# Handing the last two forward tiles of each head to the backward sweep in on-chip buffers instead of through memory

## The chip, the cores and the metric

The kernel runs on all 8 cores of one Trainium2 chip. Each core computes one sequence of the batch of 8, with the same program and no exchange between cores. The metric is the device time of the slowest core in microseconds (us).

## The reference

One hybrid encoder block on x of shape (8, 4096, 1024), float32:

```
h = adaLN(RMSNorm(x)); z = h @ W_in
hA = mlstm_scan(q, k, v, forward gates) + flip(mlstm_scan(flipped q, k, v, backward gates))   # 4 heads of 256
y  = sigmoid(gA) * (rmsnorm(hA) * mh_g * sigmoid(o)) + sigmoid(gB) * spatial_gating(u, v)
x += gate1 * (y @ W_out)
x += gate2 * (relu(adaLN(RMSNorm(x)) @ W1)^2 @ W2);  out = RMSNorm(x)
```

What matters here is the first line of the mixer: a head's output is the sum of a forward scan and a backward scan over the same 4096 positions, and the root-mean-square norm comes after that sum.

## The kernel before, in words

The sequence is cut into 32 tiles of 128 positions. The program has three stages. The first (to about 480 us in the profile) normalises, transposes and does the spatial gating branch. The second, the head stage (about 480 to 1320 us), does the mLSTM of the four heads. The third is the channel sub-layer with its two large matrix products; it goes through the tiles from the last to the first, and its first pieces of work are mixed into the end of the head stage.

The head stage is a loop over `t`, 0 to 159, and every turn of it calls `chunk_pair`. In turn t the forward scan of head `hF = t // 32` does tile `iF = t % 32`, and the backward scan of the head before, `hB = hF - 1`, does tile `iB = 31 - t % 32`. So in the first 32 turns there is only a forward scan (pass 1), in passes 2 to 4 there are both, and in the last 32 turns (pass 5) only a backward scan. The point where `t` reaches 32, 64, 96 or 128 is called a hand-over below: tile 31 of a head is the last one that its forward scan makes and the first one that its backward scan needs, one turn later. Tile 30 is made one turn earlier and needed one turn later than that.

Inside one `chunk_pair`:

- `recur("F", ...)` writes the forward numerators into PSUM bank 4 with TensorE, updates the state `Chat` on VectorE and its scaled bf16 copy `Cbf` on ScalarE. `recur("B", ...)` does the same for the backward scan with bank 5 (its `Cbf` on GpSimd, in pass 5 on ScalarE).
- For the backward tile, TensorE also makes the output gates into bank 3 from the weights `wog` (1 MB per head, loaded by `load_og`), ScalarE takes a tanh, and GpSimd makes the product `y2`.
- VectorE makes the reciprocals of the denominators of both directions with two operations and a RECIPROCAL (L1085 to L1087).
- Line 1090: ScalarE scales bank 4 by the reciprocal into the buffer `hfo[t % 2]` (float32, 128x256). Line 1091: SyncE's queue stores it to `hf_d`, in memory (128 KB).
- Line 1059: SyncE's queue loads the forward result of the backward tile from `hf_d` into `hfi[t % 3]` (128 KB).
- Line 1093: VectorE adds bank 5, scaled, to `hfi[t % 3]`, giving `hs`. ScalarE squares it (L1096, into `mxo`), GpSimd makes the reciprocal root, VectorE makes the product `mxo` (L1099), and SyncE's queue stores `mxo` to `mixa_d` (L1101).

Beside each turn, TensorE, VectorE and ScalarE do a quarter of a block of the projections of the coming blocks (`prep_part`), through pass 4. In pass 5 there are no projections left.

The order of the instructions on each engine isn't the order of the source. A planner (`Sched.schedule`) gives each operation an assumed duration and places it by the time at which its inputs are ready in that assumed time, earliest rank first among those that are ready. The ranks follow the source. A DMA is assumed to take 3 us plus its bytes at 280 GB/s, and transfers of one queue follow each other. The order so found is fixed in the program; on the chip each engine works through its own list and waits wherever an input isn't there yet. Waits are written as semaphore waits ahead of the instruction, on SyncE's queue as well. A planned order depends on all planned times before it.

Helpers record nearly all operations, so the lines of the profile are theirs: L354 is every DMA, L361 every matmul group, L373 transposes, L381 every activation, L393 and L392 tensor-scalar, L396 tensor-tensor, L401 scalar-tensor-tensor. A wait instruction has L1409 (for a DMA) or L1411 (for another engine).

Of the kernel before, what the change touches and what calls it, by code (L numbers as in the profile page):

```python
# [10 lines left out]
AF = mybir.ActivationFunctionType  # L11
# [31 lines left out]
class Sched:  # L43
# [8 lines left out]
    def R(self, *key):  # L52
        r = self.res.get(key)
        if r is None:
            r = Res(key)
            self.res[key] = r
        return r
# [188 lines left out]
def build_program(debug=False):  # L246
    nc = bass.Bass("TRN2", target_bir_lowering=False)
    SCH = Sched()
    R = SCH.R
# [33 lines left out]
    hf_d = [nc.dram_tensor(f"hf{j}_d", [S, 256], F32, kind=sk).ap() for j in range(2)]  # L283
# [8 lines left out]
    with es:  # L292
        arena = es.enter_context(nc.sbuf_tensor("arena", [128, ARENA_WORDS], F32))
        ps_all = es.enter_context(nc.psum_tensor("ps", [128, 4096], F32))[:, :]
        banks = [ps_all[:, i * 512:(i + 1) * 512] for i in range(8)]
# [3 lines left out]
        def new_dsem():  # L299
            nsem[0] += 1  # L300
            return DSem(es.enter_context(nc.semaphore(f"dsem{nsem[0]}")))
# [5 lines left out]
        def alloc(shape, dt=F32, res=(), at=None):  # L307
            n = 1
            for s_ in shape[1:]:
                n *= s_  # L310
            nb = (n * (4 if dt == F32 else 2) + 31) // 32 * 32
            if at is None:
                off = ptr[0]
                ptr[0] += nb
            else:
                off = at
            assert off + nb <= ARENA_WORDS * 4, ("arena overflow", off + nb)
            keys = [k if isinstance(k, tuple) else (k,) for k in res]
            old = []
            for r in regions:  # L320
                if r[0] < off + nb and off < r[1]:
                    assert r[2] and keys, ("no owner", shape, r)
                    old += r[2]
            regions.append((off, off + nb, keys))
            if old:
                SCH.alias(old, keys)
            ap = arena[:, off // 4:(off + nb) // 4]
            if dt != F32:
                ap = ap.bitcast(dt)
            ap = ap[:, 0:n]  # L330
            if len(shape) == 3:
                ap = ap.rearrange("p (a b) -> p a b", a=shape[1], b=shape[2])
            return ap
# [4 lines left out]
        def PB(i):  # L338
            return R("bank", i)

        def nfree(ap):
            n = 1
            for s_ in ap.shape[1:]:
                n *= s_
            return n
# [4 lines left out]
        def DMA(q, o_ap, i_ap, reads, writes, sem, pace=(), **kw):  # L350
            if q == "pool" and sem is None:
                sem = new_dsem()
            nbytes = nfree(o_ap) * o_ap.shape[0] * (4 if o_ap.dtype == F32 else 2)
            return SCH.op(q, lambda e, o_ap=o_ap, i_ap=i_ap, kw=kw: e.dma_start(out=o_ap, in_=i_ap, **kw),  # L354
                          reads, writes, dsem=sem, pace=pace, occ=0.4 if q == "sp" else 0.9, lat=3.0 + nbytes / (280e3 if q == 'sp' else 100e3))
# [22 lines left out]
        def ACTF(o_, i_, func, reads, writes, eng="act", **kw):  # L378
            t = 0.17 + nfree(o_) * 0.000833 + (0.19 if "accum_out" in kw else 0.0)
            t += 0.093 * sum(not isinstance(kw.get(n_, 1.0), float) for n_ in ("scale", "bias"))  # L380
            return SCH.op("act", lambda e, o_=o_, i_=i_, func=func, kw=kw: e.activation(o_, i_, func, **kw),  # L381
                          reads, writes, occ=t)
# [12 lines left out]
        def TT(eng, o_, a_, b_, op, reads, writes):  # L395
            return E(eng, lambda e, o_=o_, a_=a_, b_=b_, op=op: e.tensor_tensor(o_, a_, b_, op), reads, writes,  # L396
                     0.6 if op == ALU.pow else vcost(eng, o_))
# [41 lines left out]
        def hTt(kc, i):  # L439
            return hT4[:, i // 4, kc, (i % 4) * 128:(i % 4 + 1) * 128]  # L440
# [3 lines left out]
        def RH(i):  # L444
            return R("hT", i)
# [179 lines left out]
        def gpart(i):  # L625
            return int(i >= 28)
# [244 lines left out]
        hfo = [alloc([128, 256], F32, [("hfo", k)]) for k in range(2)]  # L871
        hfo_sem = [new_dsem() for _ in range(2)]
        hfi = [alloc([128, 256], F32, [("hfi", k)]) for k in range(3)]
        hfi_sem = [new_dsem() for _ in range(3)]
# [5 lines left out]
        sml = alloc([128, NSM * 8], F32, [(nm, m) for nm in ("sml", "sq") for m in range(NSM)])  # L880
# [7 lines left out]
        def RHF(hh_, i):  # L888
            return R("hf_d", hh_ % 2, i)
# [12 lines left out]
        BV, BOG, BN, BD = 2, 3, {"F": 4, "B": 5}, 6  # L902
# [144 lines left out]
        def chunk_pair(hF, iF, hB, iB):  # L1047
            t = pctr[0]
            pctr[0] += 1
            k2 = t % 2  # L1050
            so = (t % NSM) * 8
            RSM = R("sml", t % NSM)
            if hF is not None:
                recur("F", hF, iF)
            if hB is not None:
                bsl = slice(iB * 128, (iB + 1) * 128)
                k3 = t % 3
                DMA("sp", hfi[k3], hf_d[hB % 2][bsl, :], [RHF(hB, iB)], [R("hfi", k3)], hfi_sem[k3])
                recur("B", hB, iB)
                MMG([(banks[BOG][:, 0:512], hTt(kc, iB), wog[:, kc, :], kc == 0, kc == 7) for kc in range(8)],  # L1060
                    [RH(iB), R("wog")], [PB(BOG)])
                RT = R("tg", k2)
                ACTF(tg[k2], banks[BOG][:, 0:512], AF.Tanh, [PB(BOG)], [RT], scale=0.5)
                TS("dve" if hF is None else "pool", tg[k2], tg[k2], 0.5, 0.5, ALU.mult, ALU.add, [RT], [RT])
                TT("pool", y2[k2], tg[k2][:, 0:256], tg[k2][:, 256:512], ALU.mult, [RT], [R("y2", k2)])
                TT("pool", y2[k2], y2[k2], mhs[hB % 2], ALU.mult, [R("y2", k2), R("mhs", hB % 2)], [R("y2", k2)])
            iB = None if hB is None else iB
            iF = None if hF is None else iF
            aF = None if hF is None else iF * 4 + hF
            aB = None if hB is None else 128 + iB * 4 + hB  # L1070
            if aF is None:
                den, wvn, n_ = banks[BN["B"]][:, 256:257], wvi[:, aB:aB + 1], 1
                rb = [PB(BN["B"])]
                dn, rd = sml[:, so + 1:so + 2], sml[:, so + 3:so + 4]
            elif aB is None:
                den, wvn, n_ = banks[BN["F"]][:, 256:257], wvi[:, aF:aF + 1], 1
                rb = [PB(BN["F"])]
                dn, rd = sml[:, so:so + 1], sml[:, so + 2:so + 3]
            else:
                b0 = BN["F"] * 512  # L1080
                den, wvn = ps_all[:, b0 + 256:b0 + 256 + 513:512], wvi[:, aF:aB + 1:aB - aF]
                rb = [PB(BN["F"]), PB(BN["B"])]
                dn, rd = sml[:, so:so + 2], sml[:, so + 2:so + 4]
            STT(dn, den, -1.0, wvn, ALU.mult, ALU.max, rb + [R("gsc", "w", gpart(i_)) for i_ in (iF, iB) if i_ is not None], [RSM])
            STT(dn, den, 1.0, dn, ALU.mult, ALU.max, rb + [RSM], [RSM])  # L1085
            E("dve", lambda e, o_=rd, i_=dn: e.reciprocal(o_, i_), [RSM], [RSM], 0.2)  # L1086
            if hF is not None:  # L1087
                fsl = slice(iF * 128, (iF + 1) * 128)
                ACTF(hfo[k2], banks[BN["F"]][:, 0:256], AF.Copy, [PB(BN["F"]), RSM], [R("hfo", k2)], scale=sml[:, so + 2:so + 3])
                DMA("sp", hf_d[hF % 2][fsl, :], hfo[k2], [R("hfo", k2)], [RHF(hF, iF)], hfo_sem[k2])  # L1090
            if hB is not None:
                STT(hs[k2], banks[BN["B"]][:, 0:256], sml[:, so + 3:so + 4], hfi[k3], ALU.mult, ALU.add,
                    [PB(BN["B"]), RSM, R("hfi", k3)], [R("hs", k2)])
                RS2 = R("sq", t % NSM)
                ACTF(mxo[k2], hs[k2], AF.Square, [R("hs", k2)], [R("mxo", k2), RS2], accum_out=sml[:, so + 4:so + 5])
                TS("pool", sml[:, so + 5:so + 6], sml[:, so + 4:so + 5], 1.0 / 256.0, EPS, ALU.mult, ALU.add, [RS2], [RS2])  # L1096
                RSTD(sml[:, so + 5:so + 6], sml[:, so + 6:so + 7], RS2, RS2)
                STT(mxo[k2], hs[k2], sml[:, so + 6:so + 7], y2[k2], ALU.mult, ALU.mult,
                    [R("hs", k2), RS2, R("y2", k2)], [R("mxo", k2)])  # L1099
                DMA("sp", mixa_d[bsl, hB * 256:(hB + 1) * 256], mxo[k2], [R("mxo", k2)], [R("mixa_d", iB, hB)], mxo_sem[k2])  # L1100

        casts = []
        for j in range(2):
            for m in range(2):
# [391 lines left out]
```

How the kernel before makes its waits and increments, by code:

```python
    def replay(e, h):  # L1405
        for o in order[e]:
            for d in o.waits:
                if d.dsem is not None:
                    h.wait_ge(d.dsem.handle, d.dval)
                else:
                    h.wait_ge(esem[d.eng], d.count)
            if o.fn is None:
                if o.signal:
                    h.nop().then_inc(esem[e], 1)
                continue
            ins = o.fn(h)
            if o.dsem is not None:
                ins.then_inc(o.dsem.handle, 16)
            elif o.signal:
                ins.then_inc(esem[e], 1)
```

## Time and profile before

| | us |
|---|---|
| median of 3 runs | 2346.45 (2344.16 to 2347.35) |
| the profiled execution, its own time | 2342.24 |
| its span, core 0 (slowest) | 2340.7 |
| the other cores' spans | 2332.2 to 2339.1 |
| granted TensorE clock, mean of each core | 0.980 to 0.982 |
| TensorE matmul busy | 2211.5 |
| VectorE busy | 1414.3 |
| ScalarE busy | 1134.6 |
| GpSimd busy | 923.3 |

The span runs from the first to the last instruction of a core. The rows shown further down are all of core 0. Its own time is 1.5 us more than its span and lies 4.2 us below the median of the runs.

### The profile page before, as it was taken

To read this page: it belongs to the slowest core of one execution; us is meant where nothing else is said; L and a number is where in the kernel's file an instruction comes from. 1 tells how busy PE (TensorE), PEld (TensorE's weight loads), DVE (VectorE), ACT (ScalarE), POOL (GpSimd) and SP (SyncE) were. 2 spreads that over 40 slices of the span, in tenths; PEclk is the share of its full clock that TensorE was granted. 3 is DMA by queue.
4 is the path that set the end of the run, shared out by engine and by line. 5 is a ranking of instruction groups with operands and counts; after the bars stand their busy time and mean duration, and the time that the engine had idled before them with its cause. 6 is when DMAs were issued, how large, how long until landed. Compare 5 with 4: busy or idle time off the path is not lost.

```text
span 2340.7 us, 49311 instructions; the slowest of 8 cores (2332.2 to 2340.7 us)
## 1 busy us (share of the span) xinstructions
PE 2211.5 (94%) x15044; PEld 1337.3 (57%) x15044; DVE 1414.3 (60%) x3077; ACT 1134.6 (48%) x2291; POOL 923.3 (39%) x1153
## 2 busy tenths in 40 slices
PE   5999999999999999999868999999999999999997
PEld 1454545555666555555524566666666666666664
DVE  2768887788888778888758533343333343434433
ACT  4645554488766566666635333333333333333332
POOL 1656666111576566666656412222112222221220
PEclk7999999999999999999989999999999999999998
DMA  9544444224334544544565511110111111111100
GB/s 306 176 120 138 131 122 127 77 51 100 82 76 102 117 97 104 144 100 98 146 184 184 178 55 55 55 32 33 55 55 55 47 55 55 55 55 55 41 7 35
DMA packets 109265, 219.96 MB, mean 94 GB/s; under 512 B 15687, under 2 KB 65415, under 8 KB 102158
## 3 DMA queue, kind: packets, MB, share of 16 engines
q1 hardware_dynamic: 105006, 187.16, 25.3%
q0 software_dynamic: 4000, 29.66, 8.2%
q8 instruction: 124, 2.03, 0.4%
q14 instruction: 135, 1.11, 0.2%
HBM read 196.08 MB, written 79.71 MB: 118 GB/s over the span
## 4 chain that ended last, share of the span: by engine, by line
PE 76%; DVE 8%; issue 6%; DMA 4%; POOL 3%; ACT 2%; SPq 1%; DVEq 0%; POOLq 0%; ACTq 0%
PE ps L361 74%; DVE arena L401 5%; POOL arena L396 2%; PE ps L373 2%; ACT arena L381 1%; DMA arena<-x 1%; DVE arena L396 1%; DMA arena<-w_ada 1%; DMA arena<-wg_d 1%; SPq L354 1%; DMA mixa_d<-arena 1%; DVE arena L656 0%; DMA arena<-wsT 0%; POOL arena L393 0%; DVEq L1411 0%
## 5 line engine op out<-in xcount | busy, mean ns | idle before, releaser
L361 PE MATMUL ps<-arena 128*128 128x256 bf16 (+6 forms) x14020 | 2168.1, 321 | 95.6 <-DVE arena L401 34.7
L361 PEld LDWEIGHTS ps<-arena 128*128 128x128 bf16 (+1 forms) x14020 | 1276.4, 98 | 946.8 <-issue 183.9
L396 POOL TENSOR_TENSOR arena<-arena 128x1 f32<-128x1 f32 (+3 forms) x647 | 694.4, 1081 | 1056.4 <-ACT arena L381 353.9
L401 DVE SCALAR_TENSOR_TENSOR arena<-ps,arena 128x256 bf16<-128x256 f32 (+6 forms) x1474 | 606.4, 414 | 615.7 <-ACT arena L381 480.0
L381 ACT ACTIVATE arena<-ps 128x256 f32<-128x256 f32 (+2 forms) x974 | 495.2, 522 | 837.7 <-PE ps L361 702.0
L381 ACT ACTIVATE arena<-arena 128x256 bf16<-128x256 f32 (+6 forms) x566 | 405.4, 725 | 244.6 <-DVE arena L401 92.5
L381 ACT ACTIVATE arena<-ps,arena 128x512 f32<-128x512 f32 (+3 forms) x512 | 252.3, 519 | 106.6 <-DVE arena L396 31.3
L401 DVE SCALAR_TENSOR_TENSOR arena<-arena 128x256 bf16<-128x256 f32 (+4 forms) x259 | 277.9, 1074 | 30.9 <-POOL arena L396 17.9
L396 DVE TENSOR_TENSOR arena<-ps,arena 128x512 bf16<-128x512 f32 (+4 forms) x298 | 170.8, 580 | 106.1 <-PE ps L361 102.1
L393 POOL TENSOR_SCALAR arena<-arena 128x1 f32<-128x1 f32 (+2 forms) x317 | 152.8, 483 | 143.5 <-ACT arena L381 107.3
L401 DVE SCALAR_TENSOR_TENSOR arena<-arena,ps 128x514 f32<-128x514 f32 x240 | 178.7, 745 | 27.7 <-PE ps L361 24.8
L373 PE MATMUL ps<-arena 128*128 128x128 bf16 x1024 | 80.4, 223 | 17.7 <-POOL arena L396 7.7
L373 PEld LDWEIGHTS ps<-arena 128*128 128x128 bf16 x1024 | 67.1, 100 | 40.2 <-issue 22.0
L393 DVE TENSOR_SCALAR arena<-arena 128x1 f32<-128x1 f32 (+1 forms) x128 | 35.4, 278 | 60.2 <-ACT arena L381 60.0
L396 DVE TENSOR_TENSOR arena<-arena 128x2 f32<-128x2 f32 (+4 forms) x170 | 63.1, 373 | 11.7 <-ACT arena L381 3.4
L354 POOL DMA_DIRECT2D wq_d<-w_qkv x48 | 25.9, 540 | 84.1 <-DVE arena L1086 37.4
L656 DVE BATCH_NORM_STATS2 arena<-arena 128x6 f32<-128x512 f32 x64 | 44.2, 690 | 24.5 <-ACT arena L381 24.2
L392 DVE TENSOR_SCALAR arena<-arena 128x1 f32<-128x1 f32 (+5 forms) x72 | 31.0, 430 | 19.8 <-DMA arena<-bsp 12.6
L381 ACT ACTIVATION_READ_ACCUMULATOR arena<-arena 128x1 f32 x226 | 42.7, 189 | 0.0
L393 DVE TENSOR_SCALAR arena<-ps,arena 128x128 bf16<-128x128 bf16 x128 | 37.7, 337 | 2.1
L971 POOL CAST arena<-arena 128x4 bf16<-128x4 f32 x64 | 13.4, 223 | 64.6 <-DVE arena L396 37.7
L1086 DVE RECIPROCAL arena<-arena 128x2 f32<-128x2 f32 (+1 forms) x160 | 26.3, 164 | 15.3 <-DVE arena L401 0.9
(17 smaller groups left out, 90.3 us busy)
## 6 DMA issues: line engine op xcount, KB each, us to landing
arena<-x SPq DMA_DIRECT2D x64, 512.0 KB, 4.9
arena<-w_ada SPq DMA_DIRECT2D x8, 2048.0 KB, 11.5
hf_d<-arena SPq DMA_DIRECT2D x128, 128.0 KB, 3.4
arena<-hf_d SPq DMA_DIRECT2D x128, 128.0 KB, 2.9
w_d<-w POOLq DMA_DIRECT2D x32, 512.0 KB, 6.4
out<-arena SPq DMA_DIRECT2D x30, 512.0 KB, 3.5
arena<-w_d SPq DMA_DIRECT2D x13, 1024.0 KB, 5.6
arena<-w_vum SPq DMA_DIRECT2D x12, 1024.0 KB, 16.8
```

Source lines behind the costliest of these rows:

```text
L354: return SCH.op(q, lambda e, o_ap=o_ap, i_ap=i_ap, kw=kw: e.dma_start(out=o_ap, in_=i_ap, **kw), reads, writes, dsem=sem, pace=pace, occ=0 ...
L361: ins = e.matmul(o_, l_, r_, start=st, stop=sp)
L373: ins = e.transpose(o_, i_, ident)
L381: return SCH.op("act", lambda e, o_=o_, i_=i_, func=func, kw=kw: e.activation(o_, i_, func, **kw), reads, writes, occ=t)
L392: return E(eng, lambda e, o_=o_, i_=i_: e.tensor_scalar(o_, i_, s1, None, op0), reads, writes, t)
L393: return E(eng, lambda e, o_=o_, i_=i_: e.tensor_scalar(o_, i_, s1, s2, op0, op1), reads, writes, t)
L396: return E(eng, lambda e, o_=o_, a_=a_, b_=b_, op=op: e.tensor_tensor(o_, a_, b_, op), reads, writes, 0.6 if op == ALU.pow else vcost(eng, ...
L401: e.scalar_tensor_tensor(o_, a_, sc, b_, op0, op1), reads, writes, vcost("dve", o_))
L656: E("dve", lambda e, o_=st2[:, sb + hh * 6:sb + hh * 6 + 6], i_=gv[kv][:, cs]: e.bn_stats(o_, i_), [R("gv", kv, hh)], [R("st2", i % 4, hh) ...
L971: E("pool", lambda e, o_=vS[nm][k_][:, :, 256], i_=gsc["u" + nm][:, c0:c0 + 13:4]: e.tensor_copy(o_, i_), [R("gsc", "u", int(b == 7))], [R ...
L1086: E("dve", lambda e, o_=rd, i_=dn: e.reciprocal(o_, i_), [RSM], [RSM], 0.2)
```

## The change

For tiles 30 and 31 of each head, the forward result is no longer stored to `hf_d` and loaded back. ScalarE writes it directly into the `hfi` buffer that the backward scan of the next pass reads. The activation itself is the same (bank 4 scaled by the reciprocal) and moves to the end of `chunk_pair`, behind the operations of the backward tile in rank. It is no longer tied to the buffers `hfo` and their stores, but to the chosen `hfi` buffer and whoever read it last. For tile 30 of heads 1 to 3 the chosen buffer is the one that the backward sum of the same turn reads. The loads and stores of all other tiles stay.

```diff
             if hB is not None:
                 bsl = slice(iB * 128, (iB + 1) * 128)
                 k3 = t % 3
-                DMA("sp", hfi[k3], hf_d[hB % 2][bsl, :], [RHF(hB, iB)], [R("hfi", k3)], hfi_sem[k3])
+                if iB < 30:
+                    DMA("sp", hfi[k3], hf_d[hB % 2][bsl, :], [RHF(hB, iB)], [R("hfi", k3)], hfi_sem[k3])
                 recur("B", hB, iB)
...
             if hF is not None:
                 fsl = slice(iF * 128, (iF + 1) * 128)
-                ACTF(hfo[k2], banks[BN["F"]][:, 0:256], AF.Copy, [PB(BN["F"]), RSM], [R("hfo", k2)], scale=sml[:, so + 2:so + 3])
-                DMA("sp", hf_d[hF % 2][fsl, :], hfo[k2], [R("hfo", k2)], [RHF(hF, iF)], hfo_sem[k2])
+                if iF >= 30:
+                    turn_f.append((hF, iF, so, RSM))
+                else:
+                    ACTF(hfo[k2], banks[BN["F"]][:, 0:256], AF.Copy, [PB(BN["F"]), RSM], [R("hfo", k2)], scale=sml[:, so + 2:so + 3])
+                    DMA("sp", hf_d[hF % 2][fsl, :], hfo[k2], [R("hfo", k2)], [RHF(hF, iF)], hfo_sem[k2])
...
+            while turn_f:
+                hF_, iF_, so_, RSM_ = turn_f.pop()
+                kd = (32 * (hF_ + 1) + 31 - iF_) % 3
+                ACTF(hfi[kd], banks[BN["F"]][:, 0:256], AF.Copy, [PB(BN["F"]), RSM_], [R("hfi", kd)], scale=sml[:, so_ + 2:so_ + 3])
+
+        turn_f = []
```

## Rows read from the trace of the kernel before

**Rows 1.** The page: busy time by engine, the clock slices, and the end chain.
```profile
PE 2211.5 (94%) x15044; PEld 1337.3 (57%) x15044; DVE 1414.3 (60%) x3077; ACT 1134.6 (48%) x2291; POOL 923.3 (39%) x1153
...
PE 76%; DVE 8%; issue 6%; DMA 4%; POOL 3%; ACT 2%; SPq 1%; DVEq 0%; POOLq 0%; ACTq 0%
```
**Rows 2.** Windows of passes 2 to 4: window, length, busy us by engine, clock, DMA.
```profile
620.00:785.00 165.00, 162.53 (x1099) 99.48 (x1097) 138.80 (x310) 111.86 (x228) 116.82 (x209) 1.00 0.44 100
...
805.00:980.00 175.00, 164.43 (x1107) 100.32 (x1104) 141.03 (x315) 113.58 (x233) 110.56 (x199) 0.99 0.48 109
...
1000.00:1170.00 170.00, 158.97 (x1044) 95.38 (x1042) 136.82 (x304) 111.47 (x230) 110.89 (x198) 0.99 0.50 115
```
**Rows 3.** Windows around the four hand-overs, same columns.
```profile
600.00:620.00 20.00, 19.78 (x133) 12.24 (x134) 17.03 (x41) 14.60 (x30) 10.14 (x20) 1.00 0.40 89
...
788.00:803.00 15.00, 14.82 (x86) 8.31 (x87) 10.49 (x27) 9.16 (x20) 8.57 (x17) 0.89 0.45 97
990.00:1005.00 15.00, 15.00 (x100) 8.92 (x99) 11.88 (x24) 9.56 (x19) 7.93 (x15) 1.00 0.63 130
1184.00:1199.00 15.00, 10.88 (x52) 4.44 (x51) 6.37 (x16) 4.30 (x10) 4.88 (x9) 0.96 0.46 146
```
**Rows 4.** Tile hf_d: its DMA issues (ns min/median/max), and who waited for them.
```profile
L354 SPq DMA_DIRECT2D hf_d<-arena x128: 319/383/4067, 489.1 to 1189.6; - x128
L354 SPq DMA_DIRECT2D arena<-hf_d x128: 319/320/2561, 600.5 to 1305.8; - x128
...
  ACT arena L381: 5.2, 1
  DVE arena L401: 2.8, 1
```
**Rows 5.** Chain of waits at the fourth hand-over: start us, us, what.
```profile
1168.28 13.79 DMA arena<-wg_d
...
1189.62 5.90 DMA hf_d<-arena
...
1195.66 2.48 DMA arena<-hf_d
```
**Rows 6.** Timeline there: start us, us, engine, line, operation, shapes, [idle before <-releaser].
```profile
1182.20 6.11 PE L361 MATMUL ps<-arena 128*128 128x512 bf16 x25 [4.02 <-DMA arena<-wg_d]
1182.51 0.47 ACT L381 ACTIVATE arena<-ps,arena 128x256 f32<-128x256 f32 x1 [5.25 <-DMA hf_d<-arena]
...
1183.17 0.42 ACT L381 ACTIVATE arena<-arena 128x256 bf16<-128x256 f32 x1 [0.18 <-DMA mixa_d<-arena]
...
1187.17 0.47 ACT L381 ACTIVATE arena<-ps,arena 128x256 f32<-128x256 f32 x1 [0.99 <-DVE arena L1086]
...
1188.44 0.42 ACT L381 ACTIVATE arena<-arena 128x256 bf16<-128x256 f32 x1 [0.80 <-DMA mixa_d<-arena]
...
1189.29 0.16 DVE L1086 RECIPROCAL arena<-arena 128x1 f32<-128x1 f32 x1
...
1198.22 0.48 DVE L401 SCALAR_TENSOR_TENSOR arena<-ps,arena 128x256 f32<-128x256 f32 x1 [2.81 <-DMA arena<-hf_d]
...
1198.85 0.49 PE L361 MATMUL ps<-arena 128*128 128x257 bf16 x3 [1.94 <-DVE arena L401]
```
**Rows 7.** Windows from the fourth hand-over on, same columns as rows 2.
```profile
1188.00:1209.00 21.00, 13.60 (x56) 5.46 (x56) 11.43 (x30) 7.67 (x18) 8.86 (x16) 0.84 0.53 170
1209.00:1230.00 21.00, 15.95 (x94) 7.60 (x92) 16.61 (x45) 10.68 (x25) 13.79 (x24) 1.00 0.57 171
1230.00:1310.00 80.00, 70.55 (x400) 37.09 (x401) 67.89 (x165) 44.55 (x103) 53.58 (x84) 0.98 0.56 179
```
**Rows 8.** Timeline of the second hand-over, ScalarE and VectorE.
```profile
784.12 0.42 ACT L381 ACTIVATE arena<-arena 128x256 bf16<-128x256 f32 x1 [3.09 <-DMA mixa_d<-arena]
...
789.02 0.46 ACT L381 ACTIVATE arena<-ps,arena 128x256 f32<-128x256 f32 x1
789.45 0.42 ACT L381 ACTIVATE arena<-arena 128x256 bf16<-128x256 f32 x1
```

## The prediction

> **What bounds the kernel now.** Read the page's busy times and its end chain first: TensorE is busy for 94% of the span and carries 76% of the chain [rows 1]. So a change pays only where TensorE stands idle, and the question is where that is. The windows over the head stage answer it. Passes 2, 3 and 4 leave TensorE idle for 165 - 162.53 = 2.5 us, 175 - 164.43 = 10.6 us and 170 - 158.97 = 11.0 us [rows 2]. Then look at the four hand-overs, the only places that the change touches. In their windows TensorE is idle for 0.22 us of 20, 0.18 of 15, 0.00 of 15 and 4.12 of 15 [rows 3]. The first three have the store and the load too, but projections of coming blocks fill the time; the fourth opens pass 5, which has no projections left. The tile view says the same from the other side: of 256 stores and loads of `hf_d`, two were ever waited for by an engine, a ScalarE activation for 5.2 us and a VectorE sum for 2.8 us [rows 4], and the timeline puts both at the fourth hand-over [rows 6]. Last, the chain of waits there goes through the store (5.90 us) and the load (2.48 us) of tile 31 [rows 5].
>
> **The change part by part.**
>
> *Eight stores and eight loads go* (4 heads, 2 tiles). That is 16 x 128 KB = 2 MB of the head stage's traffic and 16 issues of 0.32 to 0.38 us on SyncE's queue [rows 4], about 5.5 us of a queue that isn't the bound. I count 0 for them by themselves. What matters is who waits.
>
> *Hand-overs 1 to 3: 0 us.* With the store and load gone, the sum of tile 31 can run some microseconds sooner. TensorE had at most 0.22 us idle there, so all three together can give back 0.22 + 0.18 + 0.00 = 0.4 us at most. I take 0.
>
> *Hand-over 4, the wait for tile 31.* The store was issued at 1189.62 and landed 5.90 us later, the load was issued at 1195.66 and took 2.48 us, and the sum ran at 1198.22, after VectorE had idled 2.81 us for it [rows 5, 6]. What else does that sum need? Its reciprocal, at 1189.29 for 0.16 us [rows 6], and bank 5, which the reciprocal's own inputs read before. So without the round trip it can run at about 1189.6, or 1198.22 - 1189.6 = 8.6 us sooner. That is the ceiling of this step. It isn't the gain, because TensorE went on working during the wait (output gates of coming tiles, which need only `hT` and `wog`), and this work is no longer available afterwards.
>
> The gain comes from TensorE's window. From 1188 to 1209 it was busy 13.60 of 21 us; the two stretches behind it, with the same kind of turns, were busy 15.95 of 21 (76%) and 70.55 of 80 (88%) [rows 7]. The same 13.60 us of work at those densities takes 13.60 / 0.76 = 17.9 or 13.60 / 0.88 = 15.4 us: 3.1 or 5.6 us less than 21. The granted clock was 0.84 in this window against 1.00 and 0.98 behind it [rows 7], TensorE having idled ahead. 0.84 as a mean of the full and the half level means that 32% of the stretch ran at 1.2 GHz; if that were all undone, a sixth of 13.60 us, 2.2 us at most, would come on top, but the idle time for `wog` stays (below), so I take a third, 0.7 us. Ends: 3.1 and 5.6 + 2.2 = 7.8, both under the ceiling of 8.6. I take 5.0, the middle of 3.1 and 5.6 with the 0.7.
>
> *Hand-over 4, the wait for an old store.* ScalarE waited 5.25 us until 1182.51 to write tile 30's result, because `hfo` was still being stored [rows 6]. This wait goes. Nothing is gained: TensorE stood still until 1182.20 for `wog` [rows 6], a transfer issued at 1168.28 [rows 5] ahead of everything that the change removes, and the next activation in the list, the square into `mxo`, ran at 1183.17 because its own buffer's store was late by the same congestion [rows 6]. That one is next late. Count 0; the ends are 0 and 0.6 us (1183.17 - 1182.51).
>
> *The copy moves behind the backward tile.* The activation is the same 0.46 to 0.47 us [rows 6, 8]. For tile 30 it now also waits for the sum of the same turn (0.48 us, [rows 6]) since that reads the same buffer, and by rank it comes behind the square of that turn. At the second hand-over copy and square ran back to back at 789.02 and 789.45 [rows 8], so swapping them makes bank 4 free some 0.4 to 0.6 us later. The next forward tile's matmuls wait for bank 4 and can be hidden behind projections, as TensorE's idle time there is near 0. Behind the copy on ScalarE are the `Cbf` copies and tanhs; they are moved in time only by what the planner places between. At the fourth hand-over the copy of tile 31 ran at 1187.17; behind the square at 1188.44 (0.42 us and its accumulator read) it would run at about 1189.1 and end at 1189.6 [rows 6], just as the reciprocal is done. So 0 there too. Price if the cover goes: 0.5 us a hand-over, 1.5 us in all; if the square waits for its buffer's store, up to 3.09 us (784.12, [rows 8]) each.
>
> *The planner's order.* Sixteen operations with assumed times of some 3.5 us disappear, so from the first hand-over on every engine's list may come out differently. The trace of before can't show this. The nearest rows are passes of the same work in other orders: their idle times of TensorE differ by up to 11.0 - 2.5 = 8.5 us [rows 2]. So -8.5 to +8.5 us, and I take 0, since nothing in the rows gives it a sign.
>
> **Sum.** -0 - 5.0 - 0 + 0 + 0 = -5.0 us against the profiled execution's own 2342.24: 2337.2. Its own time lies 4.2 us below the median of the runs, 2346.45, so on that scale the forecast is 2341.4 us. A difference under 0.2% (4.7 us) can't be told from no change here; the forecast lies just beyond that line.
>
> The Trainium skill bears on the price of the round trip. Here the store took 5.90 us and the load 2.48 us, 8.38 together [rows 5]. The page DMA: Bandwidth & Descriptors, section Anatomy of one DMA, gives about 2.0 us fixed plus the bytes at 436 GB/s, which for 128 KB would be an estimate of 2.3 us each and 4.6 us together. The load agrees, the store doesn't. By the page's price tile 31's sum would come at most 4.6 us sooner, and with the same discount for work done during the wait the result would be about 2344, within what can't be told from no change; the trace has the longer time, so it decides.
>
> **Rivals.**
>
> *A: given back within pass 5.* The last pass ends where VectorE and the weights' loads allow it, and the start hardly matters. For it: behind the hand-over VectorE is as busy as TensorE, 16.61 of 21 and 67.89 of 80 us (79% and 85%), and the loads of `hf_d` run on at (1305.8 - 1195.7) / 31 = 3.6 us a tile, near a pace of its own [rows 4, 5, 7]. At that pace the five tiles from 1187 on end at about 1205, when they really ended by 1209 or so: 2 to 4 us of gain remain, and later waits take more. Against it: VectorE isn't over 85% busy. Time on the median's scale: 2344 to 2347, no change measurable.
>
> *B: the new order is worse (slower).* From the first hand-over on the planner interleaves projections and scans differently, and TensorE meets its inputs late as in passes 3 and 4 rather than as in pass 2. Place: pass 2, from 620 to 785 us, the only one with an order this tight. Price: up to 8.5 us [rows 2]; it decides once the loss exceeds the 5.0 us of the hand-over by 4.7, which asks for more than this pass alone, so for a loss in pass 5 too. Time: 2352.
>
> *C: ScalarE's list (slower too).* The copy sits behind a square that waits for the store of `mxo`. Three hand-overs with 3.09 us each [rows 8] are 9.3 us less the 5.0: 2351. It decides only where such a wait meets the very turn with tile 30; in the rows of before it was one turn earlier. The page TensorE: Matmul & The Clock Gate of the Trainium skill, specification table ahead of the first section, has ScalarE's queue as strictly first in first out, so nothing could overtake the square; the ACT rows at 1182.51 and 1183.17 agree.
>
> *D: more than forecast.* The sum freed at 1189.6 keeps the clock up and the new order removes part of the 10.6 and 11.0 us of passes 3 and 4 as well: 8.6 us at the hand-over plus 2 to 4: 2335.
>
> **How the numbers follow.** Forecast 0.45 (itself spread over 3 to 8 us, a fifth of it under the line of 4.7), A 0.27, B 0.11, C 0.04, D 0.13. Faster by over 0.2%: 0.45 x 0.8 + 0.13 = 0.49. Same: 0.09 + 0.27 = 0.36. Slower: 0.15. The range goes from D's 2335, a little under, to 2350, which takes in A and the near half of B and C: 2334 to 2350. The forecast alone would be 2338 to 2344.
>
> **What would show it.** In the changed kernel the stores and loads of `hf_d` are 120 each, no wait of VectorE for them at the fourth hand-over, and the chain there no longer goes through `hf_d`. TensorE's wait for `wog` of about 4 us stays. The window of 21 us from the first matmul of pass 5 on should be busy 16 us or more with the clock near 1.0. The windows of hand-overs 1 to 3 should stay within 0.5 us. Passes 2 to 4 should be as long as before within 2 us each; if one is longer or shorter by more, the order did it (B, D). If the sum of tile 31 comes 8 us earlier, but the last load of `hf_d` less than 2 us earlier, it is A. The prediction is wrong if the hand-over returns nothing, or if passes 2 to 4 move by more than it.

## The result, and the profile after

The changed kernel takes 2324.1 us (median of 4 runs, 2320.1 to 2324.8) against 2345.3 us before. The ratio is 0.9908, with a 95% interval of 0.9892 to 0.9924: 21 us faster. The prediction said 2341.4, 5 us faster, and its range ended at 2334. The sign was right; the size was a quarter of the real one. In one run or another some executions were disturbed on one die; they are left out of all comparisons here, which is why a few kernels rest on few runs, and why the stages of one kernel below (the changed one with a reciprocal reckoned at 0.25 us) are those of its four undisturbed cores.

The page of the changed kernel, core 0, answers to [rows 1]: busy time, and the chain that ended last.

```profile
span 2323.0 us, 48997 instructions; the slowest of 8 cores (2314.0 to 2323.0 us)
...
PE 2185.5 (94%) x14771; PEld 1335.7 (57%) x15044; DVE 1401.3 (60%) x3077; ACT 1136.6 (49%) x2291; POOL 923.1 (40%) x1153
...
PE 79%; DVE 8%; issue 6%; DMA 2%; ACT 2%; POOL 1%; SPq 1%; DVEq 0%; ACTq 0%; POOLq 0%
```

The share of DMA in the chain fell from 4% to 2%. (273 matmul records are missing in this trace, so its idle times are slightly too long.) The tile view of `hf_d`, against [rows 4]:

```profile
L354 SPq DMA_DIRECT2D hf_d<-arena x120: 319/384/2312, 485.8 to 1173.3; - x120
L354 SPq DMA_DIRECT2D arena<-hf_d x120: 319/320/3866, 597.7 to 1292.5; - x120
its engine sat idle before it (us, times) until:
who waited for it (us, times):
```

There are 120 stores and 120 loads, and on this core no engine waits for any of them (on the others there are two such waits, of 1.0 and 2.5 us, both of ScalarE). Then the windows, against [rows 3] and [rows 7]: the four hand-overs, pass 5 in two parts, and the 60 us behind it (columns: busy time of TensorE, its weight loads, VectorE, ScalarE, GpSimd; clock; DMA).

```profile
600.00:620.00 20.00, 19.89 (x133) 12.21 (x134) 16.62 (x40) 13.96 (x28) 11.59 (x20) 1.00 0.32 62
786.00:801.00 15.00, 13.18 (x85) 7.54 (x85) 11.33 (x30) 9.43 (x22) 9.57 (x18) 1.00 0.49 119
985.00:1000.00 15.00, 14.89 (x91) 8.17 (x92) 9.89 (x23) 9.72 (x20) 7.52 (x15) 1.00 0.37 75
1184.00:1199.00 15.00, 11.67 (x61) 5.65 (x63) 12.18 (x33) 8.47 (x21) 8.83 (x17) 1.00 0.56 173
...
1187.00:1210.00 23.00, 17.17 (x96) 8.43 (x99) 19.54 (x56) 12.69 (x28) 15.27 (x26) 1.00 0.62 195
1210.00:1301.00 91.00, 80.81 (x465) 42.85 (x471) 73.77 (x190) 50.78 (x121) 64.13 (x100) 0.98 0.55 174
1301.00:1361.00 60.00, 57.63 (x388) 38.65 (x396) 21.56 (x55) 17.24 (x46) 10.57 (x11) 0.97 0.39 116
```

The same stretches of the kernel before, from the first turns of pass 5 on:

```profile
1189.00:1224.00 35.00, 24.12 (x114) 10.31 (x114) 22.06 (x57) 14.37 (x32) 16.71 (x32) 0.90 0.59 184
1224.00:1316.00 92.00, 79.39 (x457) 41.84 (x458) 77.99 (x187) 50.30 (x117) 64.41 (x98) 0.98 0.52 166
1316.00:1376.00 60.00, 58.16 (x385) 37.86 (x384) 21.34 (x53) 16.36 (x45) 8.56 (x12) 0.94 0.37 118
```

The first eight turns of pass 5 took 35 us and now take 23. In them TensorE is idle for 5.8 instead of 10.9 us, and its granted clock is 1.00 instead of 0.90. Of the prediction's signs, the 21 us from the first matmul of pass 5 on (1187.07) are busy for 16.24 us at a clock of 1.00, as it asked. The window of hand-over 2 didn't stay within 0.5 us: TensorE is idle there for 1.8 instead of 0.2 us (core 0).

To cut the whole span into stages, take the start of the RECIPROCAL of each turn (160 of them in every trace). The table has the median over the 8 cores of each kernel's profiled execution, in us. The last two rows are TensorE's idle time and the time at the half clock (1.2 GHz) for the two main kernels.

| stage | before | after | difference |
|---|---|---|---|
| up to turn 0, pass 1 (turns 0 to 32) | 604.2 | 604.5 | +0.3 |
| pass 2 (32 to 64) | 193.2 | 193.5 | +0.3 |
| pass 3 (64 to 96) | 197.7 | 194.1 | -3.6 |
| pass 4 (96 to 128) | 190.1 | 189.9 | -0.2 |
| turns 128 to 136 | 35.4 | 22.8 | -12.6 |
| turns 136 to 159 | 92.4 | 91.3 | -1.1 |
| the rest | 1022.6 | 1020.0 | -2.6 |
| TensorE idle, in pass 3 / turns 128 to 136 / whole | 10.8 / 11.1 / 129 | 4.9 / 5.5 / 116 | -5.9 / -5.6 / -13 |
| half clock, in turns 128 to 136 / next 60 us after pass 5 / whole | 8.5 / 4.6 / 90 | 0 / 0 / 78 | -8.5 / -4.6 / -12 |

13 us less idle time, and 12 us less at the half clock (worth at most half of that, 6 us), make 19 of the 19.5 us that the stages add up to. 12.6 of them lie right behind the fourth hand-over, where the prediction looked. But it looked for 5. (The expectations below give pass 4 a gain of 3.2 us as well; the medians over the cores don't show it.)

### The profile page after: what moved, and what is told of

Read it like the earlier page. It is cut to its first block, busy times and chain, and to the rows that moved or that the text cites. A ratio compares the mean times of both kernels' runs of the same rounds, so it can differ in the third digit from the quotient of the medians.

```text
span 2323.0 us, 48997 instructions; the slowest of 8 cores (2314.0 to 2323.0 us)
## 1 busy us (share of the span) xinstructions
PE 2185.5 (94%) x14771; PEld 1335.7 (57%) x15044; DVE 1401.3 (60%) x3077; ACT 1136.6 (49%) x2291; POOL 923.1 (40%) x1153
## 4 chain that ended last, share of the span: by engine, by line
PE 79%; DVE 8%; issue 6%; DMA 2%; ACT 2%; POOL 1%; SPq 1%; DVEq 0%; ACTq 0%; POOLq 0%
PE ps L361 77%; DVE arena L401 5%; PE ps L373 2%; ACT arena L381 2%; DVE arena L396 1%; DMA arena<-w_ada 1%; POOL arena L396 1%; DMA mixa_d<-arena 1%; SPq L354 1%; DMA arena<-wg_d 1%; DVE arena L393 0%; DVEq L1421 0%; DVE arena L1087 0%; POOL arena L393 0%; DVE arena L656 0%
## 5 line engine op out<-in xcount | busy, mean ns | idle before, releaser
L361 PE MATMUL ps<-arena 128*128 128x512 bf16 (+7 forms) x13747 | 2141.2, 318 | 107.5 <-DVE arena L401 27.8
L381 ACT ACTIVATE arena<-arena 128x512 bf16<-128x512 f32 (+6 forms) x566 | 404.8, 726 | 235.3 <-DVE arena L401 82.2
L401 DVE SCALAR_TENSOR_TENSOR arena<-arena 128x256 bf16<-128x256 f32 (+4 forms) x259 | 270.4, 1045 | 49.1 <-POOL arena L396 37.0
```

The lines of the kernel that those rows point to most:

```text
L361: ins = e.matmul(o_, l_, r_, start=st, stop=sp)
L401: e.scalar_tensor_tensor(o_, a_, sc, b_, op0, op1), reads, writes, vcost("dve", o_))
```

## The experiments

The question after this: is it the round trip that is gone, or the order of the instructions, which the planner made anew? Two tools were made. One changes the condition of the edit (which head, which tile). The other pins the order: the planner orders one form of the program, and another form is emitted in that order.

```diff
+def build_program(debug=False):
+    plan, _ = build_graph(False, None)        # graph with the round trips: only its order is kept
+    for e in ENGS:
+        for n, o in enumerate(o for o in plan[e] if not o.is_bar):
+            pos[o.key] = (o.seg, n)
+    return build_graph(True, pos)[1]          # graph with direct hand-over, emitted in that order
...
+            if self.forced:
+                for e in ENGS:
+                    seg_order[e].sort(key=lambda o: self.forced[o.key])
```

**One hand-over at a time.** `h4_only`:

```diff
-                if iB < 30:
+                if not (iB >= 30 and hB == 3):
...
-                if iF >= 30:
+                if iF >= 30 and hF == 3:
```

> The change at the fourth hand-over alone (head 3); tiles 30 and 31 of heads 0 to 2 go through memory as before, so the planned order up to the end of pass 4 is that of before. Against before at 2345: theory R (the gain is the round trip that is gone at the fourth hand-over, with pass 5 and what follows): passes 2 to 4 as long as before, turns 128 to 136 near 23 instead of 35 us, time about 2332 (-10 to -16). Theory O (the gain is the planner's new order in passes 2 to 4): about 2342 or more, -5 at most. The prediction's size for this step was -5: 2340.

Measured: 2337.6 us, ratio to before 0.9971 (0.9961 to 0.9981), 7 us faster. Turns 128 to 136 took 26.3 us instead of 35.4, but everything behind pass 5 took 1024.7 us, 2.1 more than before. Theory R came near in the turns and not in the total.

`h123_only` is the same with `hF < 3` and `hB < 3`.

> The change at hand-overs 1 to 3 alone; the fourth goes through memory as before. Theory R: only the 7 us that passes 3 and 4 became shorter remain, 2338, and turns 128 to 136 take about 35 us. Theory O: the order carries it, 2326 to 2330, and turns 128 to 136 are near 23 us though tile 31 still makes its round trip. The prediction's step for these hand-overs was 0: 2345.

Measured: 2336.3 us, 0.9966 (0.9954 to 0.9978), 8 us faster. Pass 3 took 194.2 us, as in the changed kernel, and turns 128 to 136 took 34.2. That is what R said for it. So by their ratios the two halves give 7 and 8 us, and the whole gives 21: about 6 us are in neither, which the three intervals together make uncertain by some 5 us.

**The wait without the order.** `old_order_direct` is the diff above: all eight tiles direct, the lists of the kernel before.

> All eight tiles handed over directly, but every engine's list in exactly the order that was planned for the kernel before (planned with the round trip, which is then left out). This separates the wait from the order. Theory R: the waits alone, passes 2 to 4 unchanged (+-1 us), hand-over 4 gives 8 to 12 us: about 2334. Theory O: without the new order little is gained, 2341 to 2345.

Measured: 2345.0 us, 1.0002 (0.9992 to 1.0013). **Nothing is gained in the total.** All sixteen transfers are gone, and the time is that of before. That is a balance of stages. Turns 128 to 136 fell by 2.8 us only, to 32.6, and passes 2 and 3 by 0.7 and 1.2; pass 4 and the later turns of pass 5 took 3.6 and 1.3 us more. Theory R, which asked for 8 to 12 us at the hand-over, falls, and so does the forecast of -5 for it.

Pass 4's loss has two places. Turns 108 to 112 took 28.7 instead of 27.1 us, far from any tile that the change touches. The last eight turns took 46.4 instead of 44.6. There ScalarE on five of the eight cores waited 1.9 to 7.0 us in turn 125 for an older store of `hf_d`, one that the change leaves in, and TensorE waited for ScalarE (core 7):

```profile
1180.39 0.48 ACT L400 ACTIVATE arena<-ps,arena 128x256 f32<-128x256 f32 x1 [6.72 <-DMA hf_d<-arena]
1181.01 1.88 PE L380 MATMUL ps<-arena 128*128 128x257 bf16 x8 [5.27 <-ACT arena L400]
```

In the kernel before, the like wait came one turn later (5.25 us, [rows 6]), under TensorE's wait for `wog`. The pinned form also isn't the pure removal of a wait: the copy of tile 30 keeps its old place in ScalarE's list, but now has to wait for the sum of its turn (2.27 us on core 7).

The timeline shows why the fourth hand-over gave so little (core 7, the slowest; start us, us, engine, line, operation, shapes, [idle before <-releaser]). First ScalarE's copy of tile 31, then VectorE's list:

```profile
1191.92 0.48 ACT L400 ACTIVATE arena<-ps,arena 128x256 f32<-128x256 f32 x1 [0.93 <-DVE arena L1109]
```

```profile
1194.10 0.16 DVE L1109 RECIPROCAL arena<-arena 128x1 f32<-128x1 f32 x1
1194.20 0.43 DVE L412 TENSOR_SCALAR arena<-arena 128x512 f32<-128x512 f32 x1
1195.15 0.86 DVE L420 SCALAR_TENSOR_TENSOR arena<-arena 128x256 bf16<-128x256 f32 x1 [0.52 <-POOL arena L415]
1195.93 0.74 DVE L420 SCALAR_TENSOR_TENSOR arena<-arena,ps 128x514 f32<-128x514 f32 x1
1196.71 0.46 DVE L412 TENSOR_SCALAR arena<-arena 128x512 f32<-128x512 f32 x1
1199.72 0.43 DVE L412 TENSOR_SCALAR arena<-arena 128x512 f32<-128x512 f32 x1 [2.56 <-ACT arena L400]
1200.07 0.48 DVE L420 SCALAR_TENSOR_TENSOR arena<-ps,arena 128x256 f32<-128x256 f32 x1
```

Tile 31's result is in its buffer at 1192.4, and the RECIPROCAL starts at 1194.1. The sum is the last line, 6.0 us later. Five operations stand ahead of it in the list, and one of them waits 2.56 us for ScalarE, for the gates of the tile that comes three turns later. The planner, which reckoned with the round trip, put them there. The changed kernel's list at the same place:

```profile
1187.67 0.17 DVE L1087 RECIPROCAL arena<-arena 128x1 f32<-128x1 f32 x1
1187.95 0.48 DVE L401 SCALAR_TENSOR_TENSOR arena<-ps,arena 128x256 f32<-128x256 f32 x1
...
1190.73 0.16 DVE L1087 RECIPROCAL arena<-arena 128x1 f32<-128x1 f32 x1
1191.00 0.48 DVE L401 SCALAR_TENSOR_TENSOR arena<-ps,arena 128x256 f32<-128x256 f32 x1
```

The sum comes 0.28 us behind the reciprocal and the next turn 3.1 us after this one. The same reading for all kernels and hand-overs, as the time from the start of the turn's reciprocal to the start of the sum, with the place of the sum behind it in VectorE's list (medians over the cores; 1 is right behind; the two last columns are the steps of the reciprocals):

| kernel | hand-over 1 | 2 | 3 | 4 | turn 128 to 129 | turns 128 to 136 |
|---|---|---|---|---|---|---|
| before | 5.3 (9) | 2.8 (6) | 6.4 (8) | 9.0 (6) | 10.9 | 35.4 |
| old_order_direct | 5.3 (9) | 2.8 (6) | 6.3 (8) | 6.0 (6) | 8.5 | 32.6 |
| h4_only | 5.3 (9) | 3.0 (6) | 6.8 (8) | 0.8 (2) | 2.9 | 26.3 |
| h123_only | 0.3 (1) | 0.3 (1) | 0.3 (1) | 8.2 (6) | 10.0 | 34.2 |
| new_order_memory | 4.3 (1) | 5.5 (1) | 0.4 (1) | 7.2 (1) | 10.0 | 31.1 |
| after | 0.3 (1) | 0.3 (1) | 0.3 (1) | 0.3 (1) | 3.1 | 22.8 |

In the old order the sums of hand-overs 1 to 3 run as late without the memory trip as with it.

**The order without the missing wait.** `new_order_memory` turns it round: the lists of the changed kernel, with store and load put back into SyncE's list where the copy ends.

```diff
+    plan, _ = build_graph(True, None)
...
+            pos["store", h, i] = (o.seg, o.fin + 0.35, 0)
+            pos["load", h, i] = (o.seg, o.fin + 0.35, 1)
+    return build_graph(False, pos)[1]
```

> The reverse: every engine's list in the order planned for the changed kernel, but the eight tiles go through memory again, each store and load put back into SyncE's list right where the copy is planned to end. Theory R: the round trip costs at the fourth hand-over what the change gave, and some at the others since the order doesn't reckon with it: 2336 to 2350. Theory O: 2324 to 2329, the order gives the gain with or without memory. Passes 3 and 4 should keep their 3.6 and 3.2 us under either, if the order made these.

Measured: 2347.7 us, 1.0014 (1.0002 to 1.0026): 3 us slower than before, by an interval that only just leaves out no change. Passes 2 and 3 took 198.1 and 201.8 us, 4.6 and 7.7 more than in the changed kernel, and turns 128 to 136 took 31.1 instead of 22.8. So pass 3 didn't keep its gain. Its tile view, columns as above:

```profile
who waited for it (us, times):
  DVE arena L425: 19.7, 4
  ACT arena L405: 5.8, 1
```

VectorE now waits at each of the four hand-overs (4.1, 6.8, 0.5 and 8.3 us on this core, 19.7 in all), where in the kernel before it waited once for 2.8 us [rows 4]. In the kernel before most of the trip is hidden inside the list.

The four cases in one square, as ratios to before: old order with memory 1, old order direct 1.0002, new order with memory 1.0014, new order direct 0.9908. Neither factor by itself shortens the total. Two reservations: the square was made for this one pair of orders, and the place of the eight stores and loads in SyncE's list was chosen by hand. SyncE's list stood still for those stores 30.4 us in all, so a part of what the trip costs in the new order can be that place and not the trip; it wasn't tested.

**Which tile.** `new_order_mem31` and `new_order_mem30` put only one of the two tiles through memory, in the order of the changed kernel (`through(h, i)` is `i == 31` or `i == 30`).

> The order of the changed kernel, with tile 31 alone through memory at all four hand-overs (tile 30 direct). With both tiles through memory this order took 24.5 us more than with none. Theory 31: tile 31 is needed one turn after it is made and carries nearly all of it, 18 to 25 us more than the changed kernel's 2324: 2342 to 2349. Theory Q (SyncE's list stands still behind each store, whichever tile): about half, 2336.

> The order of the changed kernel, with tile 30 alone through memory. Theory 31: tile 30 has three turns to make its trip and costs 0 to 4 us: 2324 to 2328. Theory Q: about half of the 24.5 us: 2336.

Measured: 2339.4 us with tile 31 through memory (its interval against before, 0.9951 to 1.0022, is wide because one of seven runs took 2359.7), and 2328.9 with tile 30 (0.9928, 0.9899 to 0.9957; two runs only). So 15 and 5 us over the changed kernel's 2324.1, together 20 of the 24. The waits for `hf_d` say the same: VectorE waited 11.8 us in three waits with tile 31 and never with tile 30. Tile 31 carries most, as theory 31 has it, though less than the 18 us that it named. What tile 30 costs is not a wait of an engine for its data; half of it lies in turns 128 to 136 (25.3 instead of 22.8 us), and it is a little more than the 0 to 4 us of theory 31. SyncE's list stood still for its stores 15.6 us in all, which would delay the other transfers; that this is the cause wasn't tested.

**Do hand-overs add up in a fixed order?** `new_order_mem_h4`: the new order, both tiles through memory at the fourth hand-over alone.

> The order of the changed kernel, tiles 30 and 31 through memory at the fourth hand-over alone. If the hand-overs add up: turns 128 to 136 take 31 instead of 23 us, passes 2 and 3 stay at 193.5 and 194 us, 8 us more than the changed kernel: 2332. If the trips at hand-overs 1 to 3 did no harm in this order, all of it comes here: 2345.

Measured: 2334.3 us, on two runs and without an interval, about 10 us over the changed kernel. Passes 2 and 3 stayed at 192.9 and 194.4 us and turns 128 to 136 took 32.4. In this order the hand-overs add up: about 10 here and 12.3 in passes 2 and 3.

**Do hand-overs 1 to 3 matter in an order planned for their trips?** `h4_order_direct` has all tiles direct, in the order of `h4_only`.

> All tiles direct, in the order that was planned for the kernel with the change at the fourth hand-over alone (2338). It separates, for hand-overs 1 to 3, the trip from the order. Theory W (trips at 1 to 3 cost in any order, as they cost 4.6 and 7.7 us in passes 2 and 3 of the new order): 2326 to 2330. Theory P (an order planned with the trips holds work in their place, so that leaving them out gives nothing): 2336 to 2340, passes 2 and 3 within 1.5 us of 193.4 and 197.8.

Measured: 2339.3 us, 0.9977 (0.9966 to 0.9988), against 2337.6 for `h4_only`. Passes 2 and 3: 193.5 and 197.0 us. Theory P holds. Again pass 4 grew, from 190.7 to 193.5 us, and in the same two places as in `old_order_direct`: turns 108 to 112 by 1.2 us and the last eight by 1.3. What delays turns 108 to 112 stays open.

**How much of it is the draw?** Any change before the first hand-over gives other lists from there on. The duration that the planner reckons for a RECIPROCAL was changed from 0.20 to 0.15 and to 0.25 us, in both kernels. The operations of each pair are those of before and after.

```diff
-            E("dve", lambda e, o_=rd, i_=dn: e.reciprocal(o_, i_), [RSM], [RSM], 0.2)
+            E("dve", lambda e, o_=rd, i_=dn: e.reciprocal(o_, i_), [RSM], [RSM], 0.15)
```

> The kernel before with one planning assumption changed: a reciprocal is reckoned at 0.15 instead of 0.20 us. The program's operations are the same, every engine's list from early in pass 1 on is another. Theory L (orders are a lottery; the change drew a good one): this lands anywhere within about 10 us of 2345, with passes 2 to 4 and pass 5 differing by some us each. Theory S (the planner's order fits the program; each order is about as good): within 3 us of 2345.

> The changed kernel with the same assumption of 0.15 us. Theory L: the difference to its partner isn't -21 but something between -20 and +5. Theory S: -21 +-5 against its partner, again with turns 128 to 136 at 23 to 26 us instead of about 35.

> The kernel before with a reciprocal reckoned at 0.25 us: a second draw. Theory L: within about 10 us of 2345, elsewhere than the first draw. Theory S: within 3 us of 2345.

> The changed kernel with 0.25 us. Theory L: against its partner anything from -20 to +5; the turns 128 to 136 gain 9 to 12 us in any case, since the step at the fourth hand-over falls from about 11 to 3 us whenever the planner knows that tile 31 is there; the rest changes sign. Theory S: -21 +-5.

| planner reckons a reciprocal at | before | after | difference | turns 128 to 136 | passes 2 and 3 | turn 136 to the end |
|---|---|---|---|---|---|---|
| 0.20 us (as given) | 2345.3 | 2324.1 | -21.2 | 35.4 to 22.8 | 390.9 to 387.6 | 1115.0 to 1111.3 |
| 0.15 us | 2348.7 | 2340.5 | -8.2 | 39.9 to 28.1 | 391.6 to 391.9 | 1114.6 to 1117.2 |
| 0.25 us | 2349.7 | 2347.3 | -2.4 | 34.9 to 32.5 | 392.6 to 392.6 | 1119.3 to 1119.9 |

The ratios to the given kernel before are 1.0016 and 0.9981, 1.0021 and 1.0007, each within 0.0014 at 95%, so that the -2.4 can't be told from no change. The two changed kernels moved as theory L has it, and the two kernels before ended 3.4 and 4.4 us away, just outside theory S's 3 us. One part of theory L failed: it had turns 128 to 136 gain 9 to 12 us in any case, and at 0.25 us they gained 2.4. What comes back in each draw is the step from turn 128 to 129 alone: 10.9, 12.2 and 10.8 us before, 3.1, 3.1 and 3.0 after, a gain of 7.8 to 9.1. What follows is luck: in the given order the next seven steps are 2.8, 2.8, 3.1, 2.9, 2.3, 3.4 and 2.4 us, in the order for 0.25 us they are 2.8, 5.9, 2.7, 2.9, 5.7, 3.0 and 6.7. Outside that one step the three differences are -13.4, +0.9 and +5.4 us. Over three draws the change is worth 11 us in the mean, and the given one is the best of the three by far.

## Why the prediction was wrong, point by point

**What bounds the kernel, and where.** Right. TensorE's idle time was the measure, the fourth hand-over the place, and with the lists fixed hand-overs 1 to 3 gave little: `h4_order_direct` against `h4_only` shows passes 2 and 3 at 193.5 and 197.0 against 193.4 and 197.8 us, and `old_order_direct` against before 0.7 and 1.2 us less, somewhat over the 0.4 us that the prediction allowed.

**"So without the round trip it can run at about 1189.6."** This is the step that failed first. It asked which inputs the sum needs and not where the sum stands in its engine's list. In the old order it stands six places behind its reciprocal, and with the trip gone it still runs 6.0 us late. The wait of 2.81 us in [rows 6] was only what was left of a trip of 8.4 us behind the five operations; this trace shows the part of the latency that the order did not fill. With the list fixed, 2.8 us went from these turns, not 5.0, and as much was lost elsewhere; with the new list it was 12.6. The forecast lay between the two by reasoning that fits neither.

**The size at the fourth hand-over: -5.0.** Measured -12.6 with the new list, beyond the stated ceiling of 8.6. The ceiling was that of one sum, and the one step from turn 128 to 129 kept it: -7.8. The other 4.8 us are in the seven turns behind, which have a list of their own: steps of 3.8, 4.8 and 4.3 us in the old order (the fourth, sixth and eighth) became 3.1, 2.3 and 2.4. In the other two draws these seven turns gained 2.9 and lost 5.4 us, so as far as three draws show, they are luck and not the hand-over. The granted clock was counted at 0.7 us. The time at half clock in these turns fell by 8.5 us and behind pass 5 by 4.6 us, worth at most 4.3 and 2.3 us, with the idle time ahead of it shorter.

**TensorE's wait for `wog` of 4 us stays.** It didn't: 0.6 us in the changed kernel. TensorE's waits there from 1150 to 1210 (total us, times, longest us):

```profile
PE ps L361 <- ACT arena L381: 11.8, 7, 8.7
...
PE ps L361 <- DMA arena<-wg_d: 0.6, 1, 0.6
```

The load landed 7.2 to 8.3 us ahead of turn 128's reciprocal before and 11.3 to 12.9 us ahead of it now, a shift that the new order made. ScalarE instead waited 8.1 us for a store of `mxo` in pass 4, and TensorE 8.7 us for ScalarE. That is why pass 4 gained nothing: its first 24 turns took 142.0 instead of 145.3 us, its last eight, where this wait lies, 47.3 instead of 44.6.

**The copy behind the square.** Right in the size. In the changed kernel the copy of tile 30 ran at 1178.15, behind a square that had waited 1.76 us for the store of its own buffer. Rival C's mechanism was there, once, with 1.8 us instead of 3.09, and it decided nothing. The row of ScalarE's waits for such stores in the changed kernel, from 1150 to 1200 (total us, times, longest us), has the 8.1 us of pass 4 as its longest:

```profile
ACT arena L381 <- DMA mixa_d<-arena: 11.1, 3, 8.1
```

**"The planner's order: -8.5 to +8.5 us, and I take 0, since nothing in the rows gives it a sign."** This was the wrong step that mattered: a term of the sum put at nothing, which came out at about -13 us (the -21.2 without the -7.8 of the one step). Its bound was too narrow: outside that step the three draws lie between -13.4 and +5.4. And the order was entered as a disturbance independent of the wait. The square of four cases says that for the given pair of orders it isn't: 0.0002, 0.0014 and together -0.0092. The order planned with the latency carries other work in its place, and of the four cases only the order planned without it, on a program without it, was faster. In pass 3, where the trace of before shows no wait for `hf_d` on core 0 and no more than 3.4 us in one piece on others, the new order took TensorE's idle time from 10.8 to 4.9 us; rival D named this ("removes part of the 10.6") and got 0.13. That the given order came out so much better than the other two draws is luck, which the prediction's rows could not have told.

**Rivals.** A (given back within pass 5) happened in part with the list fixed: 1.3 of the 2.8 us came back there. B and C, slower, didn't come; B's price of 8.5 us was of the right size or less, and its sign wrong. D had the right parts and a time of 2335, 11 us short. The sum of the largest terms given in the prediction, 8.6 at the hand-over and 8.5 for the order, would have been 17 us; the range ended at 2334 because they were not thought of as coming together.

## What to carry to other kernels

Where each engine has a fixed list made by a planner, a latency that is taken out needn't be worth the wait that the trace shows, but what the planner's new list makes of it. Look up how far behind its last input each consumer of the removed transfer runs (here 5.3, 2.8, 6.4 and 9.0 us, with 6 to 9 places between), not only which of them shows a wait. And before a gain of a per cent is put down to an edit, plan both versions once or twice with a slightly changed assumption: here the same edit gave -21, -8 and -2 us.

## What was not expected of the hardware

- TensorE's clock gave back up to a third of the gain (an estimate: half of the 12 us below, of 19). The mean granted clock of the first eight turns of pass 5 was 0.90 before and 1.00 after, and the 60 us behind pass 5 went from 0.94 to 0.97 on core 0; half-clock time fell by 12 us over the whole program.
- Stores and loads of `hf_d` (128 KB), which take 1.7 us at best and 3.2 in the median, took up to 13.4 us in the kernel before and 13.6 in the changed one (core 0), both in the last turns of pass 4, beside weight loads of up to 1 MB; the store of tile 31 took 5.90 us [rows 5]. The page DMA: Bandwidth & Descriptors of the Trainium skill, section Anatomy of one DMA, would put each at an estimate of 2.3 us, by a fit that it gives for transfers issued from GpSimd. The ones here are issued from SyncE; the fastest took less than that, and the median more.
